# Score products of two attention heads: the queries' high part laid twice, the keys' high part over the low part

## The reference, cut to what matters

```python
z = h @ w_in[l] + b_in[l]
q, k, v, c_a, c_b, g_a, g_b = jnp.split(z, splits, axis=-1)
...
    sc = jnp.einsum("bnqhd,bknjhd->bhnqkj", q_r, k_r).astype(jnp.float32) * scale
    sc = jnp.where(mask, sc + bias[None], NEG)
    p = jax.nn.softmax(sc.reshape(...), axis=-1)
    o = jnp.einsum("bhnqkj,bknjhd->bnqhd", p, v_r)
```

## Time and profile before

| | us |
|---|---|
| median of 3 runs | 2634.8 (2634.1 to 2635.11) |
| profiled execution, its own time | 2635.55 |
| its span in the trace | 2633.8 |
| TensorE busy | 2587.9 (98%) |
| VectorE busy | 1439.3 (55%) |
| ScalarE busy | 595.1 (23%) |
| GpSimd busy | 845.7 (32%) |

### The profile page before, as it was taken

How to read it: one execution, slowest core, us unless ns; L and a number is a source line. 1 busy time by engine, 2 the same in 40 slices (tenths; PEclk the granted TensorE clock), 3 DMA queues, 4 the chain that set the end, 5 groups by cost and what they waited for, 6 DMA issues and landing times.

```text
span 2633.8 us, 36938 instructions
## 1 busy us (share of the span) xinstructions
PE 2587.9 (98%) x14553; PEld 2117.5 (80%) x14553; DVE 1439.3 (55%) x1495; ACT 595.1 (23%) x779; POOL 845.7 (32%) x453
## 2 busy tenths in 40 slices
PE   8999998999999999999999999999999999999997
PEld 7788886788888888887777788888888888888886
DVE  6655555434444434348777787354555555555555
ACT  4234433310101010114233321311211111111113
POOL 2222222333333333333322223333333333333334
PEclk9999999999999999999999999999999999999998
DMA  6111112111211111111311111113111111111111
GB/s 210 41 32 32 40 32 94 51 45 54 56 54 55 51 48 48 48 48 56 106 38 38 38 32 49 48 49 112 48 49 48 48 48 48 48 48 48 48 48 72
DMA packets 201595, 145.11 MB, mean 55 GB/s; under 512 B 14095, under 2 KB 183738, under 8 KB 200506
## 3 DMA queue, kind: packets, MB, share of 16 engines
q1 hardware_dynamic: 189604, 122.92, 15.3%
q10 hardware_dynamic: 11926, 21.28, 2.3%
HBM read 131.59 MB, written 14.36 MB: 55 GB/s over the span
## 4 chain that ended last, share of the span: by engine, by line
PE 88%; DVE 8%; issue 2%; ACT 1%; DVEq 0%; DMA 0%; SPq 0%; ACTq 0%
PE psum L658 61%; PE psum L677 17%; PE psum L1078 3%; PE psum L697 1%; DVE h_lo L1691 1%; DVE ffn_gate L2246 1%; PE psum L785 1%; PE psum L1006 1%; DVE x_t L1945 1%; PE psum L1192 1%; PE psum L987 1%; DVE sq_sum L1686 1%; DVE ffn_val L2250 0%; DVE ffn_gate L2250 0%; DVE ffn_val L2246 0%
## 5 line engine op out<-in xcount | busy, mean ns | idle before, releaser
L615 POOL CAST w_hi<-w_raw 128x1024 fp32r<-128x1024 f32 x212 | 237.1, 1118 | 1705.7 <-issue 834.2
L658 PE MATMUL psum<-h_hi,w_hi 128*128 128x512 f32 x2256 | 712.0, 396 | 10.8 <-DVE h_lo L1794 7.2
L658 PE MATMUL psum<-h_lo,w_hi 128*128 128x512 f32 x2256 | 699.0, 390 | 0.0
L658 PE MATMUL psum<-h_hi,w_lo 128*128 128x512 f32 x2256 | 698.1, 389 | 0.0
L617 POOL TENSOR_TENSOR w_lo<-w_raw,w_hi 128x1024 fp32r<-128x1024 f32 x212 | 571.3, 2695 | 17.0
L658 PEld LDWEIGHTS psum<-h_hi,w_hi 128*128 128x128 f32 x2256 | 417.6, 188 | 106.1 <-issue 19.5
L658 PEld LDWEIGHTS psum<-h_hi,w_lo 128*128 128x128 f32 x2256 | 423.8, 188 | 89.4
L658 PEld LDWEIGHTS psum<-h_lo,w_hi 128*128 128x128 f32 x2256 | 423.8, 188 | 89.3
L1945 DVE TENSOR_TENSOR x_t<-x_t,psum 128x512 f32<-128x512 f32 x416 | 281.5, 684 | 196.0 <-PE psum L677 193.9
L2238 DVE TENSOR_TENSOR ffn_z<-psum,rinv 128x1024 f32<-128x1024 f32 x44 | 53.9, 1224 | 275.2 <-PE psum L658 267.3
L677 PE MATMUL psum<-mlp_hi,w_hi 128*128 128x512 f32 x480 | 186.7, 389 | 0.0
(11 more groups left out here) (304 smaller groups left out, 2831.9 us busy)
## 6 DMA issues: line engine op xcount, KB each, us to landing
w_raw<-in_w_up SPq DMA_DIRECT2D x152, 256.0 KB, 3.1
w_raw<-in_w_in SPq DMA_DIRECT2D x124, 256.0 KB, 3.1
w_raw<-in_w_down SPq DMA_DIRECT2D x108, 256.0 KB, 2.7
w_raw<-in_w_out SPq DMA_DIRECT2D x32, 256.0 KB, 3.1
x_in<-in_x SPq DMA_DIRECT2D x8, 512.0 KB, 8.7
x_spill<-x_t ACTq DMA_DIRECT2D x1, 4096.0 KB, 12.3
x_spill<-x_t ACTq DMA_DIRECT2D x4, 1024.0 KB, 5.2
x_t<-x_spill ACTq DMA_DIRECT2D x1, 4096.0 KB, 15.6
```

The source lines that it names most:

```text
L615: pool.tensor_copy(hi, w_raw[:, slot, :]).then_inc(weight_hi, 1)
L658: last = pe.matmul(psum[:, first_bank + t, :], w, a[:, k, t * HALF:(t + 1) * HALF], start=(k == 0 and j == 0), stop=(k == KT - 1 and j == 2))
```

## The change

`q_hi` gives way to `q_twice`, two tiles side by side. Tile j holds the high part of head j's queries twice, once in partitions 0 to 63 and once in 64 to 127. `k_hi` and `k_lo` give way to `k_parts`, also two tiles: tile j holds the high part of head j's keys in the head's own 64 partitions, and the low part in the other 64. One matmul over all 128 partitions of tile j then sums high by high and high by low. The third product, low by high, stays a matmul of 64 partitions. A group thus takes four matmuls, in the order head 0 (128), head 0 (64), head 1 (128), head 1 (64), and each head's second one signals. ScalarE copies q's high part four times (64 partitions each) and k's twice; VectorE subtracts twice for each. The two new tiles take 4 KB a partition more than the three old ones; the tiles behind them in the arena move up by that.

```diff
-        (sig_cb, q_hi, q_lo, k_hi, k_lo, v_t, ...) = arena(
-            ("sig_cb", [P, CT, SEQ], F32), ("q_hi", [P, SEQ], F32R), ("q_lo", [P, SEQ], F32R),
-            ("k_hi", [P, SEQ], F32R), ("k_lo", [P, SEQ], F32R), ("v_t", [P, SEQ], F32),
+        (sig_cb, q_twice, q_lo, k_parts, v_t, ...) = arena(
+            ("sig_cb", [P, CT, SEQ], F32), ("q_twice", [P, 2, SEQ], F32R), ("q_lo", [P, SEQ], F32R),
+            ("k_parts", [P, 2, SEQ], F32R), ("v_t", [P, SEQ], F32),
@@ scores @@
-                for i, (q, k) in enumerate(((q_hi, k_hi), (q_hi, k_lo), (q_lo, k_hi))):
-                    for j in range(2):
-                        rows = slice(DH * j, DH * (j + 1))
-                        done = pe.matmul(psum[:, 4 + j, 0:n * P], q[rows, queries], k[rows, keys],
-                                         start=(i == 0), stop=(i == 2))
-                        if i == 2:
-                            done.then_inc(scores_done, 1)
+                for j in range(2):
+                    rows = slice(DH * j, DH * (j + 1))
+                    pe.matmul(psum[:, 4 + j, 0:n * P], q_twice[:, j, queries], k_parts[:, j, keys], start=True, stop=False)
+                    pe.matmul(psum[:, 4 + j, 0:n * P], q_lo[rows, queries], k_parts[rows, j, keys], start=False, stop=True)\
+                      .then_inc(scores_done, 1)
@@ ScalarE, each pair @@
-                act.activation(q_hi[:, :], qk32[:, :], ACT.Copy).then_inc(q_hi_ready, 1)
+                for j in range(2):
+                    own, other = slice(DH * j, DH * (j + 1)), slice(DH * (1 - j), DH * (2 - j))
+                    act.activation(q_twice[own, j, :], qk32[own, :], ACT.Copy)
+                    done = act.activation(q_twice[other, j, :], qk32[own, :], ACT.Copy)
+                done.then_inc(q_hi_ready, 1)
...
-                act.activation(k_hi[:, :], qk32[:, :], ACT.Copy).then_inc(k_hi_ready, 1)
+                for j in range(2):
+                    own = slice(DH * j, DH * (j + 1))
+                    done = act.activation(k_parts[own, j, :], qk32[own, :], ACT.Copy)
+                done.then_inc(k_hi_ready, 1)
@@ VectorE, each pair @@
-                dve.tensor_tensor(q_lo[:, :], qk32[:, :], q_hi[:, :].bitcast(F32), ALU.subtract).then_inc(q_split, 1)
+                for j in range(2):
+                    own = slice(DH * j, DH * (j + 1))
+                    done = dve.tensor_tensor(q_lo[own, :], qk32[own, :], q_twice[own, j, :].bitcast(F32), ALU.subtract)
+                done.then_inc(q_split, 1)
...
-                dve.tensor_tensor(k_lo[:, :], qk32[:, :], k_hi[:, :].bitcast(F32), ALU.subtract).then_inc(k_split, 1)
+                for j in range(2):
+                    own, other = slice(DH * j, DH * (j + 1)), slice(DH * (1 - j), DH * (2 - j))
+                    done = dve.tensor_tensor(k_parts[other, j, :], qk32[own, :], k_parts[own, j, :].bitcast(F32), ALU.subtract)
+                done.then_inc(k_split, 1)
```

More of the change, by code:

```diff
@@ L242, in two_blocks @@
         U_PAD = CONV_PAD + SEQ + CONV_PAD
-        (sig_cb, q_hi, q_lo, k_hi, k_lo, v_t, v_keys, bias_raw, prob_t, bias, near_mask, prob, qk32, u_t) = arena(
-            ("sig_cb", [P, CT, SEQ], F32), ("q_hi", [P, SEQ], F32R), ("q_lo", [P, SEQ], F32R),
-            ("k_hi", [P, SEQ], F32R), ("k_lo", [P, SEQ], F32R), ("v_t", [P, SEQ], F32),
+        (sig_cb, q_twice, q_lo, k_parts, v_t, v_keys, bias_raw, prob_t, bias, near_mask, prob, qk32, u_t) = arena(
+            ("sig_cb", [P, CT, SEQ], F32), ("q_twice", [P, 2, SEQ], F32R), ("q_lo", [P, SEQ], F32R),
+            ("k_parts", [P, 2, SEQ], F32R), ("v_t", [P, SEQ], F32),
             ("v_keys", [P, GROUPS, P], F32), ("bias_raw", [P, 2, 3, P], F32), ("prob_t", [P, 2, 2, WIN], F32),
```

## The result

| | before | changed |
|---|---|---|
| median, us | 2634.95 (4 runs) | 2689.39 (4 runs, 2687.98 to 2690.55) |
| ratio, 95% interval | 1 | 1.0205 (1.0188 to 1.0223) |
| span of the profiled execution | 2633.8 | 2686.1 |
| mean granted clock | 0.994 | 0.987 |

Slower by 2.05%, 54.4 us. The forecast was 2677.6 with a range up to 2690, so the measured 2689.39 lies inside by 0.6 us. One of the eleven runs of b_chain, further down, took 3697.83 us at a mean granted clock of 0.653; its ratio leaves that run out.

What follows compares the result with a forecast made beforehand. TensorE, with 88% of the chain, was taken to bound the kernel. Products 18.2, hidden -2.4, operand wait 23.0 and clock 4.0 sum to +42.8 us on 2635.55; the forecast median was 2677.6 us, range 2655 to 2690.

Steps and rivals of the forecast that it cites:

- products, net of what v's chain hides: TensorE's score products: +18.2 us for added streams and row changes, less 2.4 us absorbed by existing waits on v's chain.
- wait ahead of the first group: TensorE waiting for q's and k's operands before each pair's first scores: 5.75 us a pair, +23.0 us in four.
- slow clock behind it: Granted clock falling during the new TensorE waits: 0 to 1.5 us lost each, taken as 1.0, +4.0 us in all.
- What a group costs today: Score products before the change: three streams of 0.16 us and two row changes of 0.21, 0.90 us a three-tile group.
- rival 4: Score products cost by their number, 0.12 us each; two fewer in 32 groups, at most -7.7 us, 2627 us; chance 0.03.
- What a group costs afterwards: Changed score products: four streams and four row changes, 1.48 us, +0.58 a three-tile group, +0.53 with two; +18.2 us total.
- Rival 2: Row changes inside a group of score products are free: +29.6 us, 2664 us; chance 0.13.
- What is hidden: TensorE's existing waits for v's chain in each pair's second to third group absorb 2.4 us of the slower groups.
- The operands' chain: ScalarE's and VectorE's split copies of q and k finish late before the first group: TensorE waits 5.75 us a pair, +23.0.
- Rival 1: VectorE's convolution steps slip past GpSimd's subtraction and the clock holds: +30.2 us, 2665 us; chance 0.22.
- rival 3: Half-partition copies take half the time on ScalarE, TensorE's wait near nothing, only products count: about 2652 us; chance 0.06.
- The clock: After each new TensorE wait of 5.75 us, work at a lowered clock loses 0 to 1.5 us, taken as 1.0: +4.0.

Runs made afterwards that it cites:

- b_chain: Kernel before the change, with VectorE's convolution step between the read of v and the first scores of group 1 moved to group 4; 2633.99 us (0.9985 to 1.0004).
- x_tail: Changed kernel with VectorE's convolution steps moved out of the way of the operands' copies, same number of steps; 2649.31 us.
- x_order: Changed kernel with each group's four products reordered: both of 128 rows first, then both of 64; 2670.62 us.
- b_heads: Kernel before the change, with its six products of 64 rows reordered: the three of head 0, then the three of head 1; 2635.14 us.
- x_pad: Changed kernel with each head's low queries in a zero-padded tile, so all four products have 128 rows; 2670.11 us.
- x_fill: Changed kernel with 28 filler products of 512 columns ahead of the two waits before each pair's first group; 2678.62 us.
- x_copies: Changed kernel's half copies and half subtractions, but the six score products of 64 rows as in the kernel before; 2671.92 us.

## Why the prediction was right, and which terms were off

| term | forecast, us | measured, us | by |
|---|---|---|---|
| products, net of what v's chain hides | 18.2 - 2.4 = 15.8 | 14.8 | x_tail less before |
| wait ahead of the first group, four times | 23.0 | 27.4 | waits of the changed kernel |
| slow clock behind it | 4.0 | 12.2 | see below |
| sum | 42.8 | 54.4 | |

**What a group costs today: right.** Three streams of two products each; x_order and b_heads show the pairing from two sides. By the number of products (rival 4) four would have been cheaper than six, and are not.

**What a group costs afterwards: right**, +0.56 against +0.58 (4.48 less 3.92). Rival 2, free changes of rows inside a group, falls with x_pad: from one of the four products to the next are 0.37 us with a change between them (changed kernel) and 0.18 without (x_pad). The drain that the Trainium skill states (TensorEngine Tiling (Array Packing), Key Properties) is what this trace shows too, at 0.18 us a change with the load behind it, for a change of rows alone.

**What is hidden: right.** 24 x 0.56 + 8 x 0.51 = 17.5 us gross (two tiles: 4.25 against 3.74), 14.8 net, so 2.7 against the 2.4 taken.

**The operands' chain: every step came, 1.1 us short a pair.** The wait was 7.00 in the pair worked out, against 5.75. ScalarE's half copies follow 1.07 us apart, not 0.95, which is 0.36 for q's and 0.12 for k's: the row of four copies in a row was not a fair model, and the high bound of 1.06 was the value. GpSimd's subtraction cost the four steps 2.7 us rather than 2.15, as it met the second and the third of them, not the third alone. VectorE's two halves of q_lo and the step behind them took 0.2 more. Rival 1 (the steps slip past GpSimd) and rival 3 (half copies at half the price) did not come.

**The clock: the mechanism right, the size a third of the truth.** I took 1.0 us a wait from a bound of 1.5. The same work (first group and twelve products) takes 4.00 us in x_tail, and in the changed kernel 7.29, 6.50, 7.50 and 6.89 us: 12.2 us in all, of which x_fill gave back 10.8 with fillers that leave a wait of up to 0.7. The step that failed is "0 to 1.5 us each": it came from one idle time whose slow stretch ended 2.9 us after the restart (401.83 to 404.69), and here it lasted 5.2 us and more.

That idle time, read in one trace, was no bound. The same wait for h_lo stands in the changed kernel's trace, and there the clock came back 6.2 us after the restart:

```profile
402.86 1.19 PE L658 MATMUL psum<-h_hi,w_hi 128*128 128x512 f32 x2 [6.35 <-DVE h_lo L1799]
408.00:409.00 1.00, 1.00 (x4) 0.50 0.00 0
409.00:410.00 1.00, 1.00 (x6) 0.99 0.00 0
```

In the traces of all eleven other kernels here it took 5.1 to 6.2 us (5.1 in b_heads, which has the same code there as the kernel before); the trace that the forecast was read from is the one exception. x_copies, with the same four waits, lost 8.4 us by the clock and the changed kernel 12.2, so this term isn't a fixed price either. The half speed also hit the dearer score products. This term makes 8.2 of the 11.6 us that the forecast missed, the operands' chain 4.4, and the products took 1.0 back.

That 27.4 + 12.2 + 14.8 comes to the measured 54.4 is partly luck: in the traces the three add up to what the pairs lost, but the two spans differ by 52.3 us, as what lies outside the pairs differs by some us between executions. The wait and the products are good to about 1 us; the clock's term differs more, as x_copies shows.

That the time lies inside the range is partly luck too. Its upper end, 12.4 us above the forecast, was made of ScalarE's copies without overlap (+2), the clock at 1.5 a wait (+2) and a part of dearer changes of rows. The changes were not dearer; the clock (8.2 us over its term) and the operands' chain (4.4 over) took their room.

## What to carry to other kernels

Count streams and changes of tile shape, not matmuls: two products of 64 rows in different halves run side by side, so merging one of each pair into a product of 128 rows saves nothing, and each change of rows cost like another stream (0.18 us, with 384 columns). If rows are to be filled, fill them all (here with zeros), and pay for the operands with passes in places where the engine has slack: six half passes ahead of a waiting TensorE cost 10 us a pair, and nothing once other work was moved out from between them. A wait of TensorE of 7 us costs more than 7, for the clock falls in it: 2 to 3.5 us more each time here. And a price read from one place in one trace is no bound: look for the same place in every trace that there is.

## What the runs showed of the hardware that was not expected

- Products of different row halves begin together even if two products stand between them in the program (b_heads). The Trainium skill (TensorE: Matmul & The Clock Gate, Part 3, The mechanism) has matmuls start strictly in program order; by that the six products would have made five streams, and the pair 66.2 + 6 x 0.32 + 2 x 0.21 = 68.5 us, less some 0.6 that v's chain would hide. It was 66.22.
- After a wait of 7 us the granted clock stayed at 0.50 for 5.2 us of unbroken work and in the first pair for some 6.9 (from 1306.66 on, to a stretch of mean 0.72). After the wait for h_lo, 6.3 to 7.0 us, it was 2.9 us in one trace and 5.1 to 6.2 in the eleven others.

```profile
1313.00:1314.00 1.00, 1.00 (x4) 0.72 0.00 0
```

- On ScalarE four copies of 64x1024 take 1.07 us from start to start, where four of 128x1024 took 0.95: with half the partitions they were no cheaper, and followed each other 0.12 us later. What makes the 0.12 was not tried.
